# Two small SBUF regions of an mLSTM layer kernel moved to other byte addresses

## The chip, the cores and the metric

The kernel runs on one core of a Trainium2 chip. The metric is the device time of one execution in microseconds, lower being better. All data are float32; the large matmuls read their operands as fp32r, each value split into a high part and a low remainder, and three matmuls (high by low, high by high, low by high) stand for one product.

## The reference

One decoder layer of width 1024 over 2048 positions, cut to what is computed:

```python
u = rmsnorm(x, mix_norm_g)
q, k, v, o_pre, if_pre = split(u @ w_in)             # 1024 -> 512, 512, 1024, 1024, 16
h = mlstm(q, k, v, gates(if_pre))                    # 8 heads, matrix memory, chunk by chunk, with a stabiliser
y = (_rms(h) * norm_g * sigmoid(o_pre)) @ w_out
h = x + y
u = rmsnorm(h, ffn_norm_g)
out = h + (silu(u @ w_gate) * (u @ w_up)) @ w_down   # 1024 -> 2816 -> 1024
```

## The kernel before, in words

The sequence is worked in two halves of 1024 positions. Each half has four stages, one behind the other:

1. Projection. The normalised rows are turned and kept as `u_hi` and `u_lo`. The weight columns come in 12 groups; each group is seven products of a Strassen scheme (units), of 4 x 3 matmuls of 128x128 stationary weights by 512 moving columns. The weights of a unit stand in one of six slots, `pring`: ScalarE casts the high part from `raw` (L841), VectorE subtracts for the low part (L1280), TensorE multiplies (L1920, L1922, L1924). The gates' input is one more product, with the stationary `if_w` (L1938, 40 + 40 matmuls).
2. Chunks. Eight chunks of 128 positions go through the mLSTM recurrence in small matmuls (L2004 to L2105), and through the output projection with the stationary `hg_hi`, `hg_lo` and the moving `wo` (L1833 to L1835).
3. Feed. Gate and up projection, 11 groups of 14 units each, with the seven slots of `ring` as stationary operand and `u_hi`, `u_lo` or `t_op` as moving operand (L2179, L2181, L2182). Unit q uses slot q modulo 7. Slots are filled from `raw_f` (ScalarE L1107, VectorE L1671).
4. Drain. Down projection, 77 units of 12 matmuls (L2227, L2229, L2231). The stationary operand of unit e is slot e modulo 3, filled from `g_in` (ScalarE L1149, VectorE L1744), the moving one is slot 3 + e modulo 3, filled from the down weights (L1750).

Every tile has an address written out by hand. `region` hands out stretches of each partition in order, rounded up to 32 bytes, and tiles are placed at offsets in them:

```python
base = -(-nc.sbuf_base // 32) * 32
pring_at = [r_a + 12 * KB, r_q + 8 * KB, r_b + 8 * KB, r_q, r_q + 4 * KB, r_q + 12 * KB]
ring_at = [r_b + 8 * KB, r_b + 12 * KB, r_a + 12 * KB, r_q, r_q + 4 * KB, r_q + 8 * KB, r_q + 12 * KB]
t23_op = place("t23_op", r_c, [P, 2, 2, 4, NB], F32R)
```

The regions `r_u` (64 KB), `r_v` (33024 bytes) and `r_q` (33280 bytes) stand ahead of `r_a` (16 KB), `r_b` (16 KB) and `r_c` (32800 bytes), and behind these the small tiles (`state`, `ident`, `pick`, `mask` and others). `base` is 16512, which is 128 above a multiple of 256. All six regions start at 128 above a multiple of 256. Counted from `r_u` in units of 1024 bytes, `r_v` has the remainder 0, `r_q` 256, and `r_a`, `r_b` and `r_c` 768.

In `r_a` lie: the input rows `x_in` 1 to 3, `pring` slot 0, `negm`, `wint`, `cols`, `vtc`, `gain2`, `xn2`, `ring` slot 2 and three of the `kept` tiles. In `r_b`: `raw` 0, `pring` slot 2, `if_w`, `wo_raw`, half of `raw_f`, all of `g_in`, `ring` slots 0 and 1. The moving operands `u_hi` and `u_lo` lie in `r_u`, `t_op` in `r_c` and `r_v`.

Of the kernel before, what the change touches and what calls it, by code (L numbers as in the profile page):

```python
# [15 lines left out]
HEADS = 8  # L16
# [10 lines left out]
VW = DV + 1  # L27
# [94 lines left out]
def mlstm_layer(nc, x, mix_norm_g, ffn_norm_g, w_gate, w_up, w_down, w_in, b_if, norm_g, w_out, out):  # L122
# [8 lines left out]
    with ExitStack() as ctx:  # L131
# [6 lines left out]
        def region(nbytes):  # L138
            at = top[0]
            top[0] += -(-nbytes // 32) * 32  # L140
            return at
# [10 lines left out]
        KB = 1024  # L152
        r_u = region(64 * KB)
        r_v = region(TILES * HEADS * VW * 4)
        r_q = region(32 * KB + 512)
        r_a = region(16 * KB)
        r_b = region(16 * KB)
        r_c = region(28 * KB + HEADS * VW * 4)


        u_hi = place("u_hi", r_u, [P, TBS, KD, NB], F32R)
# [2111 lines left out]
```

## Time and profile before

| | before |
|---|---|
| median of 3 runs | 2180.55 us (2180.15 to 2181.9) |
| the profiled execution | 2179.42 us |
| its span, first to last instruction | 2177.8 us |
| TensorE busy | 2126.1 us, 98% |
| VectorE, ScalarE, GpSimd busy | 66%, 43%, 12% |
| mean granted TensorE clock | 0.994 |

The profiled execution is 1.6 us longer than its span (start and end outside the first and last instruction), and 1.1 us shorter than the median. The duration shown for a matmul contains its way through the pipeline; the pace of TensorE is to be read from the distances between starts.

### The profile page before, as it was taken

Reading aid. Unit: us, or ns where it says so; the run is one execution under the profiler, and the core shown is the slowest. Engines: PE = TensorE matmul, PEld = TensorE weight load, DVE = VectorE, ACT = ScalarE, POOL = GpSimd, SP = SyncE. Lnnn points to the kernel's source line nnn. Section 1 sums busy time; section 2 is a strip of 40 time slices with the busy share of each in tenths; the row PEclk is TensorE's granted clock in tenths of the full one; section 3 lists DMA queues with packets and bytes.
Section 4 is the critical chain, followed back from the end, with each engine's and each line's share of the span. In section 5 each row is a group of like instructions: output and inputs, shape, how many; then the busy total and the mean of one; then the engine's idle time right before and its main releaser. Section 6 shows DMA issues by size and latency. Waiting matters only on the chain.

```text
span 2177.8 us, 29479 instructions
## 1 busy us (share of the span) xinstructions
PE 2126.1 (98%) x10440; PEld 1766.0 (81%) x10440; DVE 1431.5 (66%) x2274; ACT 939.2 (43%) x1686; POOL 252.5 (12%) x357
## 2 busy tenths in 40 slices
PE   5999999999999999999999999899999999999999
PEld 4888878888888888788878888788888888888887
DVE  8775466686656565579687644767865756556764
ACT  4443664453333333345444346543533333333443
POOL 4111100020101010100122111001110101001000
PEclk8999999999999999999999999999999999999999
DMA  4333364213233324863524334532223332357443
GB/s 146 102 116 106 98 238 145 88 49 121 97 116 101 116 92 142 295 229 113 155 68 140 96 102 155 213 136 78 68 97 116 101 109 95 100 197 245 149 132 109
DMA packets 200289, 281.56 MB, mean 129 GB/s; under 512 B 12913, under 2 KB 131697, under 8 KB 200177
## 3 DMA queue, kind: packets, MB, share of 16 engines
q1 hardware_dynamic: 171696, 183.07, 26.6%
q0 software_dynamic: 28480, 97.02, 12.7%
q8 instruction: 68, 1.11, 0.2%
q14 instruction: 45, 0.36, 0.1%
HBM read 197.73 MB, written 82.31 MB: 129 GB/s over the span
## 4 chain that ended last, share of the span: by engine, by line
PE 89%; DVE 6%; ACT 2%; DMA 1%; issue 1%; SPq 0%; POOL 0%; DVEq 0%; POOLq 0%; ACTq 0%
PE ps L2179 13%; PE ps L2181 13%; PE ps L2182 13%; PE ps L1920 7%; PE ps L1924 7%; PE ps L1922 7%; PE ps L2227 6%; PE ps L2231 6%; PE ps L2229 6%; PE ps L1833 2%; PE ps L1835 2%; PE ps L1834 2%; PE ps L1840 1%; DMA g_in<-ops_hbm 1%; PE ps L2098 1%
## 5 line engine op out<-in xcount | busy, mean ns | idle before, releaser
L1671 DVE TENSOR_TENSOR ring<-raw_f,ring 128x512 fp32r<-128x512 f32 x308 | 211.4, 687 | 187.6 <-ACT ring L1107 186.5
L1107 ACT CAST ring<-raw_f 128x512 fp32r<-128x512 f32 x308 | 191.1, 622 | 208.0 <-PE ps L2182 194.0
L2179 PE MATMUL ps<-u_lo,ring 128*128 128x512 f32 x704 | 275.6, 391 | 2.2 <-DVE u_lo L1268 2.2
L2182 PE MATMUL ps<-u_hi,ring 128*128 128x512 f32 x704 | 274.1, 389 | 0.0
L2181 PE MATMUL ps<-u_hi,ring 128*128 128x512 f32 x704 | 273.9, 389 | 0.0
L2227 PE MATMUL ps<-ring,ring 128*128 128x512 f32 x616 | 240.9, 391 | 7.1 <-DVE ring L1750 7.1
L2229 PE MATMUL ps<-ring,ring 128*128 128x512 f32 x616 | 239.8, 389 | 0.0
L2231 PE MATMUL ps<-ring,ring 128*128 128x512 f32 x616 | 239.7, 389 | 0.0
L2179 PE MATMUL ps<-t_op,ring 128*128 128x512 f32 x528 | 205.9, 390 | 0.0
L2182 PE MATMUL ps<-t_op,ring 128*128 128x512 f32 x528 | 205.5, 389 | 0.0
L2181 PE MATMUL ps<-t_op,ring 128*128 128x512 f32 x528 | 205.4, 389 | 0.0
L1149 ACT CAST ring<-g_in 128x512 fp32r<-128x512 f32 x154 | 95.6, 621 | 223.3 <-PE ps L2231 210.4
L1744 DVE TENSOR_TENSOR ring<-g_in,ring 128x512 fp32r<-128x512 f32 x154 | 108.4, 704 | 110.5 <-ACT ring L1149 110.3
L772 POOL DMA_DIRECT2D ops_hbm<-kept x154 | 83.3, 541 | 761.3 <-DVE kept L1769 561.7
L1280 DVE TENSOR_TENSOR pring<-raw,pring 128x512 fp32r<-128x512 f32 x132 | 90.6, 690 | 110.0 <-ACT pring L841 109.2
L1764 DVE TENSOR_TENSOR kept<-ps,kept 128x512 f32<-128x512 f32 x132 | 90.9, 689 | 106.3 <-PE ps L2182 106.3
L2179 PEld LDWEIGHTS ps<-u_lo,ring 128*128 128x128 f32 x704 | 132.2, 188 | 29.6 <-DVE u_lo L1268 2.7
L2182 PEld LDWEIGHTS ps<-u_hi,ring 128*128 128x128 f32 x704 | 132.1, 188 | 27.6
L2181 PEld LDWEIGHTS ps<-u_hi,ring 128*128 128x128 f32 x704 | 132.2, 188 | 26.8
L1920 PE MATMUL ps<-u_lo,pring 128*128 128x512 f32 x384 | 151.1, 394 | 2.9 <-DVE u_lo L1268 2.8
L1924 PE MATMUL ps<-u_hi,pring 128*128 128x512 f32 x384 | 150.0, 391 | 0.0
L1922 PE MATMUL ps<-u_hi,pring 128*128 128x512 f32 x384 | 149.9, 390 | 0.0
(219 smaller groups left out, 4198.8 us busy)
## 6 DMA issues: line engine op xcount, KB each, us to landing
ops_hbm<-kept POOLq DMA_DIRECT2D x154, 256.0 KB, 2.4
g_in<-ops_hbm SPq DMA_DIRECT2D x154, 256.0 KB, 2.7
raw<-in_ml_w_in_dram SPq DMA_DIRECT2D x24, 1024.0 KB, 5.3
proj_hbm<-pkept POOLq DMA_DIRECT2D x96, 256.0 KB, 2.7
raw_f<-in_ffn_w_gate_dram SPq DMA_DIRECT2D x44, 512.0 KB, 4.7
raw_f<-in_ffn_w_up_dram SPq DMA_DIRECT2D x44, 512.0 KB, 4.5
b<-in_ffn_w_down_dram SPq DMA_DIRECT2D x88, 256.0 KB, 4.9
x_in<-in_x_dram SPq DMA_DIRECT2D x16, 512.0 KB, 6.1
```

The source lines that it names most:

```text
L1107: nc.scalar.copy(four(ring[slot][:, 0, :]), feed_source(q, s)).then_inc(w_hi_done, 1)
L1671: nc.vector.tensor_tensor(four(ring[slot][:, 1, :]), feed_source(q, s), four(ring[slot][:, 0, :].bitcast(F32)), ALU.subtract).then_inc(w_l ...
L1744: nc.vector.tensor_tensor(ring[e % 3][:, 1, :], g_in[e % 4][:, :], ring[e % 3][:, 0, :].bitcast(F32), ALU.subtract).then_inc(ea_lo_done, 1)
L1920: pe.matmul(banks(bank), w[:, 0, now], moved(kind, 1, k), start=(fresh and k == 0), stop=False, skip_group_check=True)
L1922: pe.matmul(banks(bank), w[:, 0, now], moved(kind, 0, k), start=False, stop=False, skip_group_check=True)
L1924: last = pe.matmul(banks(bank), w[:, 1, now], moved(kind, 0, k), start=False, stop=(k == 3), skip_group_check=True)
L2179: pe.matmul(banks(bank), wh, moved(kind, 1, k), start=(fresh and k == 0), stop=False, skip_group_check=True)
L2181: pe.matmul(banks(bank), wh, moved(kind, 0, k), start=False, stop=False, skip_group_check=True)
L2182: last = pe.matmul(banks(bank), wl, moved(kind, 0, k), start=False, stop=(k == 3), skip_group_check=True)
L2227: pe.matmul(banks(bank + j), a[:, 0, now], w[:, 1, :], start=(fresh and n == 0), stop=False, skip_group_check=True)
L2229: pe.matmul(banks(bank + j), a[:, 0, now], w[:, 0, :], start=False, stop=False, skip_group_check=True)
L2231: last = pe.matmul(banks(bank + j), a[:, 1, now], w[:, 0, :], start=False, stop=(n == GROUPS - 1), skip_group_check=True)
```

## The change

The starts of three regions are moved up by some bytes. Nothing else is changed: the same instructions, tiles, semaphores and orders.

```diff
-        r_a = region(16 * KB)
-        r_b = region(16 * KB)
-        r_c = region(28 * KB + HEADS * VW * 4)
+        r_a = region(192 + 16 * KB) + 192
+        r_b = region(96 + 16 * KB) + 96
+        r_c = region(224 + 28 * KB + HEADS * VW * 4) + 224
```

The paddings add up: `r_a` moves by 192 bytes, `r_b` by 192 + 96 = 288, `r_c` and every small tile behind it by 288 + 224 = 512. Counted modulo 256, `r_a` has moved by 192, `r_b` by 32, and everything else by nothing. With the regions move `ring` slots 0 and 1 (by 288), `ring` slot 2 (by 192), `pring` slot 2 and `if_w` (by 288) and `pring` slot 0 (by 192).

## Rows read from the trace of the kernel before

**Rows 1.** The page: its span, and part 1, busy time.

```profile
span 2177.8 us, 29479 instructions
...
PE 2126.1 (98%) x10440; PEld 1766.0 (81%) x10440; DVE 1431.5 (66%) x2274; ACT 939.2 (43%) x1686; POOL 252.5 (12%) x357
```

**Rows 2.** The page, part 4: the chain that ended last, by engine.

```profile
PE 89%; DVE 6%; ACT 2%; DMA 1%; issue 1%; SPq 0%; POOL 0%; DVEq 0%; POOLq 0%; ACTq 0%
```

**Rows 3.** Windows in feed and drain: us; busy and (instructions) by engine, clock, DMA.

```profile
500.00:600.00 100.00, 100.00 (x443) 82.81 (x442) 65.83 (x102) 36.75 (x63) 11.35 (x21) 1.00 0.29 96
...
1800.00:1900.00 100.00, 100.00 (x443) 82.81 (x442) 65.50 (x101) 36.37 (x62) 10.82 (x20) 1.00 0.29 94
1000.00:1080.00 80.00, 80.00 (x353) 65.74 (x352) 61.96 (x98) 39.57 (x76) 6.94 (x8) 1.00 0.49 147
2000.00:2100.00 100.00, 100.00 (x442) 82.78 (x442) 77.33 (x120) 42.26 (x74) 1.45 (x2) 1.00 0.44 137
```

**Rows 4.** Groups of TensorE instructions by line and form.

```profile
L2179 PE MATMUL ps<-u_lo,ring 128*128 128x512 f32 x704 | 275.6, 391 | 2.2 <-DVE u_lo L1268 2.2
...
L2227 PE MATMUL ps<-ring,ring 128*128 128x512 f32 x616 | 240.9, 391 | 7.1 <-DVE ring L1750 7.1
...
L2179 PE MATMUL ps<-t_op,ring 128*128 128x512 f32 x528 | 205.9, 390 | 0.0
...
L1920 PE MATMUL ps<-u_lo,pring 128*128 128x512 f32 x384 | 151.1, 394 | 2.9 <-DVE u_lo L1268 2.8
...
L1920 PE MATMUL ps<-t_op,pring 128*128 128x512 f32 x288 | 113.6, 394 | 5.4 <-DVE t_op L1268 5.3
...
L1833 PE MATMUL ps<-wo,hg_hi 128*128 128x512 f32 x256 | 103.6, 405 | 1.8 <-DVE wo L1488 1.8
...
L1938 PE MATMUL ps<-u_lo,if_w 128*128 128x512 f32 x40 | 16.0, 399 | 1.1 <-DVE u_lo L1268 1.1
```

**Rows 5.** Timeline of TensorE in the feed: start, duration, instruction.

```profile
599.61 0.39 PE L2179 MATMUL ps<-t_op,ring 128*128 128x512 f32 x1
...
600.97 0.39 PE L2179 MATMUL ps<-u_lo,ring 128*128 128x512 f32 x1
...
606.41 0.39 PE L2179 MATMUL ps<-t_op,ring 128*128 128x512 f32 x1
...
609.81 0.39 PE L2179 MATMUL ps<-t_op,ring 128*128 128x512 f32 x1
```

**Rows 6.** Timeline of TensorE in the drain.

```profile
999.73 0.39 PE L2229 MATMUL ps<-ring,ring 128*128 128x512 f32 x1
...
1009.92 0.39 PE L2229 MATMUL ps<-ring,ring 128*128 128x512 f32 x1
```

**Rows 7.** The tile ring: its weight loads, min/median/max ns.

```profile
L2179 PEld LDWEIGHTS ps<-u_lo,ring x704: 186/188/190, 461.3 to 1957.6; 128*128 128x128 f32 x176
...
L2227 PEld LDWEIGHTS ps<-ring,ring x616: 186/188/190, 889.1 to 2173.5; 128*128 128x128 f32 x154
```

**Rows 8.** Timeline of TensorE, small matmuls of two chunks.

```profile
344.55 2.05 PE L2098 MATMUL ps<-v,dmat 128*128 128x129 f32 x16
...
358.96 1.04 PE L2105 MATMUL ps<-ident,hrow 128*128 128x128 f32 x8
```

**Rows 9.** Line L1560 of VectorE, min/median/max ns.

```profile
L1560 DVE SCALAR_TENSOR_TENSOR state<-state,dec,ps x64: 339/344/352, 294.1 to 1503.1; 128x129 f32<-128x129 f32 x64
```

**Rows 10.** Who TensorE waited for, longest first.

```profile
PE ps L1840 <- DVE x_in L1244: 13.7, 4, 9.1
PE ps L2105 <- DVE hrow L1599: 8.6, 2, 4.3
PE ps L2227 <- DVE ring L1750: 7.1, 6, 2.4
```

**Rows 11.** The loads of g_in, L605: who waited, and us to landing.

```profile
  ACT ring L1149: 12.9, 2
...
DMA to landing us min/median/max: 2.4/2.7/14.6
```

**Rows 12.** The chain in a chunk stage, 285 to 440 us, by line.

```profile
by line: PE ps L1833 13.2%; PE ps L1835 13.0%; PE ps L1834 12.9%; PE ps L2098 7.7%; PE ps L2080 4.6%; PE ps L2105 4.4%; PE ps L2094 4.3%; PE ps L2016 3.5%; DVE wo L1488 3.1%; issue 2.5%; PE ps L2039 2.3%; PE ps L2004 2.1%; PE ps L2026 1.9%;
```

## The prediction

> **What bounds the kernel now.** I read the page first. TensorE is busy for 2126.1 us of a span of 2177.8 us [rows 1], and the chain that ended last is TensorE for 89% of the span, VectorE for 6%, ScalarE for 2% and DMA for 1% [rows 2]. So what counts first is the pace of TensorE, and only then what it waits for. The windows say the same by stage: in the feed and in the drain TensorE is busy without a gap, at a granted clock of 1.00 (2.4 GHz), with 442 or 443 instructions in 100 us [rows 3].
>
> The groups by line give the number of large matmuls. Each product is three lines with equal counts, of which I show one: feed 3 x (704 + 528) = 3696, drain 3 x 616 = 1848, projection 3 x (384 + 288) = 2016, output projection 3 x 256 = 768, and the gates 40 + 40 = 80 [rows 4]. That is 8408. Their pace comes from starts in the timeline: 45 distances in 599.61 to 609.81 us are 10.20 us, 226.7 ns each [rows 5]; 45 distances in the drain are 10.19 us, 226.4 ns [rows 6]. So 8408 x 0.2267 = 1906 us, 88% of the span, go at one pace. At 2.4 GHz it is 544 cycles for 512 columns. If a column takes a cycle (an estimate; no row shows less), 32 cycles, 13.3 ns, are left over in each matmul, and these are what an address could change on TensorE.
>
> **The change part by part.** No instruction, semaphore, order or byte count is changed, so there is nothing to add or take away by counting. What can change is the duration of an access whose address has another remainder. Every region began at the same remainder modulo 256. Now `r_a` is 192 off and `r_b` 32 off (and, `base` being a multiple of 64, starts no longer at a multiple of 64). I go through who touches them.
>
> *TensorE, stationary operand.* Moved are 6 of the 14 units of a feed group (slots 0, 1, 2, twice), 3696 x 6/14 = 1584 matmuls; all 1848 of the drain; 2 of 6 slots in the projection, 672; and the 80 of the gates: 4184 in all. In `r_b` are 1056 of the feed, 1248 of the drain (slots 0 and 1 in 52 of 77 units, 24 each), 336 and 80, together 2720. Of the moving operands of 512 columns none is moved modulo 256.
>
> What does the trace say of relative position? Only differences that are multiples of 256 occur among the large matmuls, but they differ among themselves. Modulo 512, `u_hi` and `u_lo` are 256 away from every `ring` slot, and `t23_op` (a part of `t_op`) is 0 away. The feed passes from `t_op` to `u_lo` and back: 6 distances on `t_op` take 1.36 us, the 24 that follow 5.44 us, the 15 after these 3.40 us, each 226.7 ns [rows 5]. The drain, whose two operands are 512 apart modulo 1024, has the same pace within 0.3 ns [rows 6]. A window of 100 us runs through all seven slots five times and has the same pace as one in the drain to 0.5% [rows 3]. The weight loads last 186 to 190 ns in all 704 and all 616 instances, whatever else ran [rows 7]. That is 38 ns less than the pace of 226.7 ns, so a load could grow by a fifth and still end under the matmul before it. A constant remainder of 32 cycles over all these pairs looks like a fixed price of a change of weights rather than like a collision that depends on low address bits. I cost this part at nothing.
>
> Both bounds of it: on the gain side all 13.3 ns on all 4184, that is 55.8 us. On the loss side the nearest row is one with starts off the usual grid, L2098, whose moving slices of 129 columns begin 516 bytes apart: 16 of them take 2.05 us, less the last one's 0.28 us is 1.77 us over 15 distances, 118 ns; the eight transposes of 128 columns with aligned operands take 1.04 - 0.27 = 0.77 us over 7, 110 ns [rows 8]. 8 ns more (one column and a change of pass are in it too) on the 2720 in `r_b` would be 21.8 us. Between nothing and these ends I take nothing, since the rows of the same form lie there.
>
> The row gives 226.7 ns from start to start. The Trainium skill, "TensorE: Matmul & The Clock Gate", section "Back-to-back issue gap", gives for an isolated matmul N/2.4 + 2.5 ns, 215.8 ns for 512 columns. The trace doesn't agree; were the 10.9 ns between them a collision that the shift ends, the sum would be 4184 x 10.9 ns = 45.6 us less, an estimate from that page. By the rows it is nothing.
>
> *VectorE and ScalarE.* They fill the moved slots and read `raw_f` 0, `g_in`, `raw` 0, `wo_raw`. VectorE is busy for 66% of a feed window and 77% of a drain window, ScalarE for about 37% and 42% [rows 3]; TensorE covers them, with slots filled ahead. Cover is gone only where a fill is waited for. TensorE's longest waits are 13.7 us for `x_in`, 8.6 us for `hrow` and 7.1 us for `ring` L1750 [rows 10]; of these `x_in` 1 to 3 and the `g_in` and slots behind the third are moved. In the chunk stage `wo` (reads `wo_raw`) is 3.1% of a chain of 155 us, 4.8 us, twice 9.6 us [rows 12]. What a start off the grid costs VectorE: the four slices of `state` are 516 bytes apart, and all 64 instances take 339 to 352 ns, 3.8% between the extremes [rows 9]. So 13.7 + 7.1 + 9.6 = 30.4 us x 3.8% = 1.2 us either way is the bound; I take 0.
>
> *DMA.* Loads of `g_in` land in 2.7 us at the median, 14.6 us at most (behind the down weights, at the start of a drain); ScalarE waits 12.9 us for them in two places [rows 11], of which TensorE feels a part of its 7.1 us. If a load to `r_b` were 5% slower, 0.05 x 14.6 = 0.7 us in each half, 1.5 us in all; I take 0.
>
> The trace doesn't split landing times by address. The Trainium skill, "DMA: Bandwidth & Descriptors", section "How a descriptor splits into AXI transactions", says that a descriptor not starting at a multiple of 256 bytes fetches from the boundary below it, in beats of 32 bytes. A row of 2048 bytes would take 68 beats before, 69 in `r_b` and 66 in `r_a`: an estimate of 0.2 us on the 14.6 us. Neither rule nor row makes more of it than noise.
>
> The sum: 2179.4 us of the profiled execution + 0 = 2179.4 us; with the 1.1 us by which the median lies above it, 2180.5 us.
>
> **The rivals.**
> 1. *The stationary reads collided with the moving ones and no longer do (faster).* For it: the 32 cycles left over, in a kernel whose operands all had one remainder modulo 256. Against it: the same pace at every multiple of 256 that occurs. Full price 55.8 us, 2124.7 us; a third of it, the likelier size as the collision would have to be partial, 18.6 us, 2161.9 us. It decides from 1.1 ns per matmul on. The weight loads might show it too.
> 2. *A start in `r_b` that is no multiple of 64 makes a weight load disturb the matmul beside it (slower).* For it: no weight load off that grid occurs before, so no row excludes it. Against it: the moving and VectorE rows at 516-byte steps. 8 ns x 2720 = 21.8 us, 2202.3 us; it decides from 1.6 ns per matmul on.
> 3. *Equal remainders were what kept the streams apart, and the shift makes them collide (slower).* Up to another 32 cycles on 4184, 2236 us. Nothing in the profile speaks for it but that other remainders are untried.
> 4. *The moved fills and landings make the waits longer (slower).* 1.2 + 1.5 = 2.7 us, 2183.2 us, which is still no measurable change; it would need 1.6 times its bound.
>
> **How the numbers follow.** A measurement of this kernel tells some 0.2%, 4.4 us, from no change. Forecast, no effect: 0.60 (rival 4 within it, 0.03 of it). Rival 1: 0.22. Rival 2: 0.13. Rival 3: 0.05. Faster 0.22, same 0.60, slower 0.18. The time is 2180.5 us; by itself the forecast's range is 2178 to 2183. For 8 in 10 I add the smaller half of rival 1 (down to 2158, 0.11) and the smaller part of rival 2 (up to 2192, 0.10), which makes 0.81.
>
> **What would show it.** In the changed kernel 45 distances in feed and drain should again be 10.2 us, and 100 us hold 442 or 443 instructions. Weight loads should stay at 188 ns. A distance other than 226.7 ns in the units of slots 0 to 2, with the old one in slots 3 to 6, would prove rival 1, 2 or 3; a drain that changed by more per matmul than the feed would too, since every unit of it is touched. Longer `L1107`, `L1671`, `L1149` or `L1744`, or longer landings of `g_in`, would be rival 4. I am wrong if low address bits matter at all to the pair of reads in TensorE: no row of this kernel tests that.

## The result, and the profile after

The changed kernel takes 2200.44 us (median of 3 runs, 2197.83 to 2202.06) against 2180.55 us: 0.88% slower, ratio 1.0088 (95% interval 1.0065 to 1.0111). The profiled execution takes 2202.06 us; its span is 2200.3 us, 22.5 us more than before. The forecast was 2180.5 us with a range up to 2192 us; the time lies above both.

The page after, its span and busy times, and of part 4 the line by engine:

```profile
span 2200.3 us, 29479 instructions
...
PE 2148.9 (98%) x10440; PEld 1768.0 (80%) x10440; DVE 1432.7 (65%) x2274; ACT 939.4 (43%) x1686; POOL 252.4 (11%) x357
...
PE 89%; DVE 6%; ACT 2%; DMA 2%; issue 1%; SPq 0%; POOL 0%; DVEq 0%; ACTq 0%; POOLq 0%
```

Beside [rows 1, 2]: the same 10440 matmuls keep TensorE busy for 22.8 us more, which is as much as the span has grown (22.5 us). VectorE has 1.2 us more, ScalarE 0.2 us, GpSimd nothing. The windows of the kernel after, with the columns of [rows 3]:

```profile
500.00:600.00 100.00, 100.00 (x438) 81.89 (x437) 65.61 (x101) 36.50 (x64) 10.81 (x20) 1.00 0.30 98
1000.00:1080.00 80.00, 80.00 (x346) 64.71 (x345) 63.81 (x103) 41.88 (x82) 5.47 (x6) 1.00 0.46 138
```

TensorE is again busy without a gap, at the same granted clock of 1.00, yet the feed window holds 438 matmuls where there were 443, and the drain window 346 where there were 353. So the matmuls themselves come at a slower pace: 1.1% in this feed window, 2.0% in this drain window. The groups by form show it weakly, since a duration contains the pipeline: after,

```profile
L2179 PE MATMUL ps<-u_lo,ring 128*128 128x512 f32 x704 | 277.6, 394 | 2.2 <-DVE u_lo L1268 2.2
L2227 PE MATMUL ps<-ring,ring 128*128 128x512 f32 x616 | 243.6, 395 | 7.7 <-DVE ring L1750 7.6
L2179 PE MATMUL ps<-t_op,ring 128*128 128x512 f32 x528 | 206.6, 391 | 0.0
...
L1833 PE MATMUL ps<-wo,hg_hi 128*128 128x512 f32 x256 | 103.5, 404 | 1.7 <-DVE wo L1488 1.7
```

means of 394, 395 and 391 ns where [rows 4] have 391, 391 and 390; L1833, whose operands did not change their remainders, stays (404 against 405). Sharper are the starts of units. In the feed after, the first matmul of the units of slots 0, 1, 2, 3, 4 and 5 of one group (timeline of TensorE), and in the drain of four units in a row, on slots 0, 1, 2 and 0:

```profile
627.00 0.39 PE L2179 MATMUL ps<-u_lo,ring 128*128 128x512 f32 x1
...
629.79 0.40 PE L2179 MATMUL ps<-u_lo,ring 128*128 128x512 f32 x1
...
632.59 0.40 PE L2179 MATMUL ps<-u_lo,ring 128*128 128x512 f32 x1
...
635.35 0.40 PE L2179 MATMUL ps<-u_lo,ring 128*128 128x512 f32 x1
...
638.09 0.39 PE L2179 MATMUL ps<-t_op,ring 128*128 128x512 f32 x1
...
640.81 0.39 PE L2179 MATMUL ps<-t_op,ring 128*128 128x512 f32 x1
...
981.64 0.40 PE L2227 MATMUL ps<-ring,ring 128*128 128x512 f32 x1
...
984.44 0.40 PE L2227 MATMUL ps<-ring,ring 128*128 128x512 f32 x1
...
987.24 0.39 PE L2227 MATMUL ps<-ring,ring 128*128 128x512 f32 x1
...
989.99 0.39 PE L2227 MATMUL ps<-ring,ring 128*128 128x512 f32 x1
```

Twelve matmuls take 2.72 us in slot 4, as everywhere before (12 x 226.7 ns), but 2.79 and 2.80 us in slots 0 and 1 (moved with `r_b`), 2.76 us in slot 2 (moved with `r_a`), and 2.74 us in slot 3, which did not move but follows slot 2. In the drain it is 2.80, 2.80 and 2.75 us. Over all units of the trace, the mean distance from start to start in ns, worked out from the starts in the two traces (distances over 300 ns left out):

```
              feed, slot 0    1      2      3      4      5      6     drain, slot 0  1      2      gates
before           226.8  226.8  226.8  226.8  226.8  226.7  226.8        226.8  227.0  226.8  227.5
after            232.8  233.4  229.6  228.5  226.8  226.7  227.5        233.0  233.2  229.9  233.1
```

The sum of these: feed (12.0 + 13.2 + 5.6 + 3.4 + 1.4 ns for the two units of each slot) x 12 x 22 groups = 9.4 us; drain 6.2 x 1248 + 3.1 x 600 = 9.6 us; projection 3.2 us in the same way; gates 0.4 us; 22.6 us in all, against 22.5 us of span. For this pair of executions nothing is left for anything else. The medians lie only 19.9 us apart, since the profiled execution before was 1.1 us below its median and the one after 1.6 us above; so a few us elsewhere, either way, are not excluded by this sum (e10 below does that). The other views agree. Weight loads after, then TensorE's waits, then landing times of `g_in`:

```profile
L2179 PEld LDWEIGHTS ps<-u_lo,ring x704: 186/188/190, 464.0 to 1973.3; 128*128 128x128 f32 x176
L2227 PEld LDWEIGHTS ps<-ring,ring x616: 186/188/192, 896.4 to 2196.0; 128*128 128x128 f32 x154
```

```profile
PE ps L1840 <- DVE x_in L1244: 13.6, 4, 9.3
PE ps L2105 <- DVE hrow L1599: 8.6, 2, 4.3
PE ps L2227 <- DVE ring L1750: 7.6, 5, 2.6
```

```profile
DMA to landing us min/median/max: 2.4/2.7/13.7
```

The loads' durations [rows 7] and the landing at its least and median [rows 11] are as they were, the three waits [rows 10] to 0.5 us; the longest landing is 0.9 us shorter. A weight load is not longer on record; what is stretched is the distance between matmuls.

### The profile page after: what moved, and what is told of

Its sections match the earlier page's. It is cut to its first block, busy times and chain, and to the rows that moved or that the text cites. A ratio compares the mean times of both kernels' runs of the same rounds, so it can differ in the third digit from the quotient of the medians.

```text
span 2200.3 us, 29479 instructions
## 1 busy us (share of the span) xinstructions
PE 2148.9 (98%) x10440; PEld 1768.0 (80%) x10440; DVE 1432.7 (65%) x2274; ACT 939.4 (43%) x1686; POOL 252.4 (11%) x357
## 4 chain that ended last, share of the span: by engine, by line
PE 89%; DVE 6%; ACT 2%; DMA 2%; issue 1%; SPq 0%; POOL 0%; DVEq 0%; ACTq 0%; POOLq 0%
PE ps L2182 13%; PE ps L2179 13%; PE ps L2181 13%; PE ps L1920 7%; PE ps L1922 7%; PE ps L1924 7%; PE ps L2227 6%; PE ps L2231 6%; PE ps L2229 6%; PE ps L1833 2%; PE ps L1835 2%; PE ps L1834 2%; PE ps L1840 1%; DMA g_in<-ops_hbm 1%; PE ps L2098 1%
## 5 line engine op out<-in xcount | busy, mean ns | idle before, releaser
L1671 DVE TENSOR_TENSOR ring<-raw_f,ring 128x512 fp32r<-128x512 f32 x308 | 211.5, 688 | 192.6 <-ACT ring L1107 192.3
L1107 ACT CAST ring<-raw_f 128x512 fp32r<-128x512 f32 x308 | 190.9, 622 | 213.1 <-PE ps L2182 205.1
L2227 PE MATMUL ps<-ring,ring 128*128 128x512 f32 x616 | 243.6, 395 | 7.7 <-DVE ring L1750 7.6
L2231 PE MATMUL ps<-ring,ring 128*128 128x512 f32 x616 | 243.0, 395 | 0.0
L2229 PE MATMUL ps<-ring,ring 128*128 128x512 f32 x616 | 243.0, 394 | 0.0
L1149 ACT CAST ring<-g_in 128x512 fp32r<-128x512 f32 x154 | 95.5, 620 | 232.5 <-PE ps L2231 218.2
L1744 DVE TENSOR_TENSOR ring<-g_in,ring 128x512 fp32r<-128x512 f32 x154 | 108.5, 705 | 119.3 <-ACT ring L1149 119.0
```

The source lines that it names most:

```text
L1107: nc.scalar.copy(four(ring[slot][:, 0, :]), feed_source(q, s)).then_inc(w_hi_done, 1)
L1671: nc.vector.tensor_tensor(four(ring[slot][:, 1, :]), feed_source(q, s), four(ring[slot][:, 0, :].bitcast(F32)), ALU.subtract).then_inc(w_l ...
L1744: nc.vector.tensor_tensor(ring[e % 3][:, 1, :], g_in[e % 4][:, :], ring[e % 3][:, 0, :].bitcast(F32), ALU.subtract).then_inc(ea_lo_done, 1)
L2227: pe.matmul(banks(bank + j), a[:, 0, now], w[:, 1, :], start=(fresh and n == 0), stop=False, skip_group_check=True)
L2229: pe.matmul(banks(bank + j), a[:, 0, now], w[:, 0, :], start=False, stop=False, skip_group_check=True)
L2231: last = pe.matmul(banks(bank + j), a[:, 1, now], w[:, 0, :], start=False, stop=(n == GROUPS - 1), skip_group_check=True)
```

## The experiments

Theory A: what counts is where the stationary operand of a large matmul lies. In form A1 it is its place relative to the moving operand, modulo some power of two; in form A2 the start of the operand itself, against a grid. Theory B: the fills and transfers into the moved regions are slower. Each ratio is to the kernel before, timed on the same chip, and the microseconds behind a ratio are worked out from it (the medians alone give 41 us for e4 and within 1 us of the figure given for the others). Diffs are against the kernel before; `...` stands for lines left out. Paces of slots are means over the distances between starts in the trace, as above.

**e1_rb32**: only `r_b` is moved modulo 256.

```diff
-        r_b = region(16 * KB)
-        r_c = region(28 * KB + HEADS * VW * 4)
+        r_b = region(32 + 16 * KB) + 32
+        r_c = region(224 + 28 * KB + HEADS * VW * 4) + 224
```

> Only r_b is moved by 32 bytes modulo 256 (the small tiles behind it by 256). Theory A, the address of the stationary operand sets TensorE's pace: the units of ring slots 0 and 1 go at 233 ns per matmul as in the changed kernel, slot 2 and all others at 226.7 ns; in all 528 x 12.8 ns in the feed, 1248 x 6.3 ns in the drain, 336 x 6.5 ns in the projection and 0.5 us for the gates, 17.3 us above the kernel before (ratio 1.008). Theory B, fills and transfers into the region are slower and TensorE waits: the pace stays 226.7 ns and the waits grow.

Measured: 2197.5 us, ratio 1.0071 (1.0055 to 1.0088), 15.5 us where 17.3 were expected. Feed slots 0 and 1 at 232.8 and 233.4 ns, slots 2 to 5 at 226.6 to 227.2 ns, drain slots 0 and 1 at 232.8 and 233.4 ns. The last distance in a unit of slot 6, the one ahead of the first matmul of slot 0, is 235 ns (226.7 ns before). The timeline shows what runs in it: the last matmul of slot 6 on `t_op`, the load of the first weights of slot 0, then their matmul.

```profile
625.46 0.40 PE L2182 MATMUL ps<-t_op,ring 128*128 128x512 f32 x1
625.47 0.19 PEld L2179 LDWEIGHTS ps<-u_lo,ring 128*128 128x128 f32 x1
625.70 0.39 PE L2179 MATMUL ps<-u_lo,ring 128*128 128x512 f32 x1
```

So the cost begins one matmul early, at the time when the first moved weights are loaded beside an unmoved matmul. The stationary operands in `r_b` alone (two `ring` slots, one `pring` slot and `if_w`) make most of the loss.

**e2_ra192**: only `r_a` is moved modulo 256.

```diff
-        r_a = region(16 * KB)
-        r_b = region(16 * KB)
+        r_a = region(192 + 16 * KB) + 192
+        r_b = region(64 + 16 * KB) + 64
```

> Only r_a is moved by 192 bytes modulo 256 (r_b and the small tiles by 256). Theory A: ring slot 2 goes at about 229.5 ns and the first matmuls of slot 3 too, pring slot 0 likewise; 2.4 us in the feed, 1.6 us in the drain, 0.9 us in the projection, 4.9 us above the kernel before (ratio 1.002). A variant of A in which only starts off a multiple of 64 cost: no change at all, ratio 1.000, since 192 is a multiple of 64.

Measured: 2183.58 us, ratio 1.0012 (1.0002 to 1.0021), 2.6 us. Slot 2 goes at 229.0 ns, its distances run 229, 232, 226 in turn; all others, slot 3 too, at 226.7 to 227. So a start that is moved by a multiple of 64 costs as well, if less, and the grid of 64 of the second rival is not the explanation. The two together (18.1 us) agree with the change (19 us by its ratio) within the intervals; slot 3, slow in the changed kernel (228.5 ns) and in neither of these two, would make 0.9 us of the difference.

**e3_all32**: everything is moved by 32 bytes.

```diff
-        base = -(-nc.sbuf_base // 32) * 32
+        base = -(-nc.sbuf_base // 32) * 32 + 32
```

> All regions and tiles together are moved by 32 bytes, so that no operand's position relative to another changes, but every start is off a multiple of 64. Theory A1, the position of the stationary operand relative to the moving one counts: pace 226.7 ns everywhere, ratio 1.000. Theory A2, the start of the stationary operand itself counts: all 8408 large matmuls pay the 6.3 ns seen in the slots of r_b, 53 us more, ratio 1.024 or above if the moving operand pays as well.

Measured: 2181.65 us, ratio 1.0006 (0.9997 to 1.0016), and the windows in feed and drain, first of the kernel before, then of this one:

```profile
560.00:660.00 100.00, 100.00 (x443) 82.81 (x442) 60.63 (x93) 37.32 (x64) 9.42 (x18) 1.00 0.33 105
960.00:1060.00 100.00, 100.00 (x441) 82.27 (x441) 83.91 (x136) 52.87 (x102) 5.48 (x6) 1.00 0.56 180
...
560.00:660.00 100.00, 100.00 (x443) 82.84 (x442) 60.39 (x93) 37.34 (x64) 9.11 (x17) 1.00 0.33 105
960.00:1060.00 100.00, 100.00 (x441) 82.30 (x440) 83.89 (x136) 52.87 (x102) 5.46 (x6) 1.00 0.56 182
```

Every operand stands 32 bytes off and nothing is slower. A2 falls; A1 stands.

**e4_scan**: one kernel with a different shift for each slot (`pring` and `if_w` likewise; the tiles behind them in `r_q` are moved by 256).

```diff
-        ring_at = [r_b + 8 * KB, r_b + 12 * KB, r_a + 12 * KB, r_q, r_q + 4 * KB, r_q + 8 * KB, r_q + 12 * KB]
+        ring_at = [r_b + 8 * KB + 64, r_b + 12 * KB + 128, r_a + 12 * KB + 96, r_q + 32, r_q + 4 * KB + 160,
+                   r_q + 8 * KB + 192, r_q + 12 * KB + 224]
...
```

> Each ring slot has its own shift modulo 256 while the moving operands of the feed stay: slot 0 64, slot 1 128, slot 2 96, slot 3 32, slot 4 160, slot 5 192, slot 6 224 bytes. The pace of each slot in the feed is read from the trace. Theory A1 with a period of 64 bytes: slots 0, 1 and 5 at 226.7 ns, slots 2, 3, 4 and 6 at 233 ns; since 192 cost 2.7 ns in the changed kernel the period should be longer, and then the slots take several paces, slot 5 about 229.5 ns and slot 3 about 233 ns. If any slot is faster than 226.7 ns, there is a version that beats the kernel before. The time is expected 30 to 60 us above before.

Measured: 2222.25 us, ratio 1.020 (1.018 to 1.022), 44 us.

```profile
560.00:660.00 100.00, 100.00 (x432) 80.70 (x431) 55.81 (x86) 36.44 (x63) 8.14 (x15) 1.00 0.32 103
960.00:1060.00 100.00, 100.00 (x430) 80.44 (x429) 82.50 (x136) 50.41 (x96) 1.47 (x2) 1.00 0.55 175
```

Every slot is slow, those at 64, 128 and 192 bytes too, so a period of 64 bytes falls. The next kernel adds finer steps, and its table has the paces of both.

**e6_fine**: the slots are views that begin some elements into their tile.

```diff
-        ring_at = [r_b + 8 * KB, r_b + 12 * KB, r_a + 12 * KB, r_q, r_q + 4 * KB, r_q + 8 * KB, r_q + 12 * KB]
-        ring = [place(f"ring{i}", at, [P, 2, NB], F32R) for i, at in enumerate(ring_at)]
+        ring_at = [r_b + 8 * KB + 224, r_b + 12 * KB + 224, r_a + 12 * KB, r_q, r_q + 4 * KB,
+                   r_q + 8 * KB, r_q + 12 * KB]
+        ring_off = (4, 7, 3, 1, 2, 4, 6)
+        ring = [place(f"ring{i}", at, [P, 2 * NB + 8], F32R)[:, o:o + 2 * NB].rearrange("p (a n) -> p a n", a=2)
+                for i, (at, o) in enumerate(zip(ring_at, ring_off))]
...
```

> Steps finer than 32 bytes: ring slot 0 is 240 bytes off modulo 256, slot 1 252, slot 2 12, slot 3 4, slot 4 8, slot 5 16, slot 6 24 (pring likewise). If what counts are pieces of 32 bytes, slots 2 to 6 stay at 226.7 ns and slots 0 and 1 go at 233 ns like 224. If any difference from 0 counts, all are slower, up to 233 ns. If a slot is faster than 226.7 ns, some of the 32 cycles above 512 are a collision that the kernel before still has; I expect none. Between 6 and 45 us more.

Measured: 2213.13 us, ratio 1.0147 (1.0129 to 1.0165), 32 us. The pace of the feed by the place of the stationary operand relative to the moving one, from the starts in both traces (fifth to eleventh distance of a unit, so that the neighbour slots weigh little), with 0 from the kernel before:

```
bytes modulo 256   0     4     8     12    16    24    32    64    96    128   160   192   224   240   252
ns per matmul    226.7 232.3 230.5 233.2 233.3 230.1 232.7 233.6 234.2 232.3 233.8 229.0 233.1 228.3 233.3
```

Zero is the only place without a cost. There is no order in the rest that I can name: 4 bytes cost 5.6 ns, 192 bytes cost 2.3 ns. None is faster than 226.7 ns. So the reading in pieces of 32 bytes falls, and the other, that any difference costs, stands. The figures are good to about 1 ns: 32 bytes reads 232.7 here and 233.3 in e8.

The drains of these two kernels have pairs in which both operands are moved. In e4 their differences are 32, 224 and 160 bytes, and the same seven distances read 233.1, 233.2 and 234.4 ns, as in the feed. In e6 they are 236 (stationary at 240, moving at 4), 244 (252 and 8) and 252 (12 and 16), and read 236.6, 231.1 and 230.3 ns, where 252 in the feed reads 233.3. So at steps of 32 bytes the difference gives the cost to about 1 ns, but at finer steps it does not give it alone; no run moves the moving operand by less than 32 bytes while the stationary one stays.

**e5_ru32**: the moving operand is moved instead.

```diff
-        r_u = region(64 * KB)
-        r_v = region(TILES * HEADS * VW * 4)
+        r_u = region(32 + 64 * KB) + 32
+        r_v = region(224 + TILES * HEADS * VW * 4) + 224
```

> Only r_u, in which the moving operands u_hi, u_lo and wo lie, is moved by 32 bytes modulo 256; no stationary operand and no ring slot is. Theory A1, the position of the stationary relative to the moving operand counts (here -32, that is 224, for which the scan showed 233 ns): the units on u_hi and u_lo go at about 233 ns in all seven slots, those on t_op and the whole drain at 226.7 ns, the output projection slower too; 4112 matmuls x 6.4 ns = 26 us more, ratio 1.012. Rival: only the place of the stationary operand counts: ratio 1.000.

Measured: 2208.95 us, ratio 1.0128 (1.011 to 1.0147), 28 us. Windows in feed and drain:

```profile
560.00:660.00 100.00, 100.00 (x434) 81.18 (x433) 55.62 (x85) 36.63 (x63) 8.12 (x15) 1.00 0.32 103
960.00:1060.00 100.00, 100.00 (x442) 82.58 (x441) 84.44 (x138) 50.58 (x97) 1.47 (x2) 1.00 0.56 182
```

The feed has 434 instead of 443, the drain is untouched. By unit: 233.3 to 233.6 ns in each of the eight of a group on `u_lo` and `u_hi`, whichever slot; of the six on `t_op`, 226.7 to 226.8 in those that follow another on `t_op`, 229.7 in those that come right behind a unit on `u_lo`. The output projection, on `wo`, goes from 228.4 to 233.1 ns. No slot was moved, and the slots are slow. The last distance of a unit on `t_op`, the one ahead of the first matmul on `u_lo`, is 226.7 ns: in it the next weights are loaded beside a moving operand that stands at the same remainder as they do.

**e7_pad256**: shifts of 256, 512 and 768 bytes.

```diff
-        r_a = region(16 * KB)
-        r_b = region(16 * KB)
-        r_c = region(28 * KB + HEADS * VW * 4)
+        r_a = region(256 + 16 * KB) + 256
+        r_b = region(256 + 16 * KB) + 256
+        r_c = region(256 + 28 * KB + HEADS * VW * 4) + 256
```

> r_a is moved by 256, r_b by 512, r_c by 768 bytes: other addresses and other places modulo 512 and 1024, but all operands have equal remainders modulo 256. Theory A1 with a period of 256: pace 226.7 ns everywhere, ratio 1.000. With a longer period (512 or 1024): the feed and the drain slower, by up to 6.5 ns on 4184 matmuls, 27 us.

Measured: 2180.5 us, ratio 1.0000 (0.9990 to 1.0010); all slots of feed and drain at 226.6 to 227.1 ns. Moves by whole multiples of 256 bytes cost nothing.

**e8_slots32**: all slots are moved by 32 bytes.

```diff
+        ring_at = [r_b + 8 * KB + 32, r_b + 12 * KB + 32, r_a + 12 * KB + 32, r_q + 32, r_q + 4 * KB + 32,
+                   r_q + 8 * KB + 32, r_q + 12 * KB + 32]
...
```

> All seven ring slots, all pring slots, if_w and one of the three hg tiles are moved by 32 bytes modulo 256, the moving operands in r_u, r_v and r_c are not. In the drain both operands are ring slots, so their relative position stays. Theory A1: feed and projection at 233 ns in every slot, the drain back at 226.7 ns, although its stationary operands stand exactly where the changed kernel has two of them; (3696 + 2016 + 80 + 288) x 6.3 ns = 38 us more, ratio 1.0176. Rival, the stationary start itself counts: the drain at 233 ns too, 50 us, ratio 1.023.

Measured: 2216.94 us, ratio 1.0164 (1.0146 to 1.0182), 36 us. Windows in feed and drain:

```profile
560.00:660.00 100.00, 100.00 (x431) 80.49 (x430) 55.56 (x86) 36.01 (x62) 8.14 (x15) 1.00 0.33 104
960.00:1060.00 100.00, 100.00 (x442) 82.56 (x441) 83.64 (x138) 51.22 (x98) 1.47 (x2) 1.00 0.56 179
```

431 in the feed, 442 in the drain. The stationary operands of the drain stand where the change put two of them, but their moving partners now stand there too, and the pace is 226.9 ns.

**e10_slots_back**: the changed kernel with the stationary operands put back and everything else in `r_a` and `r_b` left shifted.

```diff
-        r_a = region(16 * KB)
-        r_b = region(16 * KB)
+        r_a = region(192 + 16 * KB + 64) + 192
+        r_b = region(32 + 16 * KB + 224) + 32
-        ring_at = [r_b + 8 * KB, r_b + 12 * KB, r_a + 12 * KB, r_q,
+        ring_at = [r_b + 8 * KB + 224, r_b + 12 * KB + 224, r_a + 12 * KB + 64, r_q,
...
```

> The changed kernel, but with ring slots 0 to 2, pring slots 0 and 2 and if_w (with t4, which shares its place) put back to the remainder of the moving operands; raw, raw_f, g_in, wo_raw, x_in, xn2, negm, wint, cols, vtc and the kept tiles stay shifted by 32 or 192 bytes modulo 256. Theory A1, only the pair of the large matmuls' operands counts: 226.7 ns everywhere, ratio to the kernel before 1.000 (within 0.2%). Rival, the fills, transfers or small matmuls in the shifted regions hold a part of the loss: the sum of e1 and e2 (18.1 us) against the slots' 22 us leaves them at most a few us, ratio up to 1.002.

Measured: 2180.86 us, ratio 0.9995 (0.9986 to 1.0004). Windows in feed and drain:

```profile
560.00:660.00 100.00, 100.00 (x443) 82.86 (x442) 60.42 (x93) 36.83 (x64) 8.66 (x16) 1.00 0.33 105
960.00:1060.00 100.00, 100.00 (x441) 82.30 (x441) 84.11 (x136) 52.16 (x101) 5.47 (x6) 1.00 0.56 184
```

The counts are those of the kernel before. Fills, transfers and small matmuls with shifted operands cost at most 0.04% (0.9 us) by the upper end of the interval. B falls.

**e9_small_even**: the kernel before with the small tiles at the common remainder.

```diff
-        r_c = region(28 * KB + HEADS * VW * 4)
+        r_c = region(28 * KB + HEADS * VW * 4 + 224)
...
         state = small("state", [P, 4, VW])
+        region(224)
         colt = small("colt", [P, TILES, 72])
```

> The kernel before with state, colt, ident, ident_b, pick, mask and not_first moved so that they begin at the remainder of all regions too (before: 160 for state, 192 for the others, against 128). If the pair rule holds for the small matmuls of 128 columns, transposes (ident against x_in, hrow, vtc) and L2004, L2026 get cheaper; their pace of 109 ns is likely set by something else, since 192 against 128 costs nothing visible there. Expected between 0 and 3 us less, ratio 0.999 to 1.000; a gain of over 4 us would make it a version better than both.

Measured: 2179.92 us, ratio 0.9995 (0.9986 to 1.0004). No gain beyond the noise. The transposes L1840 and L2105, with `ident` 64 bytes off their other operand before and 0 here, have a median distance of 109 ns in both traces: they don't pay for this difference. Nothing in these experiments points to a version that beats the kernel before.

## Why the prediction was wrong

*What bounds the kernel* was right: the pace of TensorE in 8408 matmuls of 512 columns decides, and it did.

*TensorE, stationary operand* is the step that failed: "I cost this part at nothing", because the pace was the same for all pairs that the kernel has. All of these pairs lie a multiple of 256 bytes apart, as I had noted, and e7 shows that such pairs are alike. They were samples of one case, not of many; the argument from them to other differences had nothing under it, as the prediction's own last sentence says ("no row of this kernel tests that"). The runs put 19.9 us in its place by the medians, 22.6 us by the trace: 5.6 to 6.6 ns on each of 2720 matmuls at 32 bytes (16.8 us), 2.3 to 3.1 ns on 1464 at 192 bytes (4.1 us), and 1.7 us on unmoved units next to these. The count of 4184 affected matmuls was right, and e5 and e8 show that it was right to ask whether a moving operand moves too. The drain changed by more per matmul than the feed (5.2 against 2.5 ns), which the prediction had named as a sign of a real effect in TensorE; its slots 3 and 6 did not keep the old pace as it said, since each stands next to a moved one.

The 32 cycles in excess of 512 were read as a fixed price of a change of weights. In fifteen places tried none had less, so nothing contradicts that, and nothing shows it either. But it said nothing about what could come on top: 5.6 to 7.5 ns, 13 to 18 cycles at 2.4 GHz, at ten of the fourteen differences of the table, and 1.6 to 3.8 ns at the other four.

*Rival 2* had nearly the size (21.8 us against 20 measured), by luck: it wanted a start off a multiple of 64 to cost by itself, which e3 excludes, and had 8 ns from rows of matmuls of another form. *Rival 3*, equal remainders keep the two streams apart, is the one that e3, e5 and e8 bear out; I gave it 0.05 and its full price, 32 more cycles, where the runs show 13 to 16 at 32 bytes and 5 to 7 at 192. *Rival 1* is excluded at every place tried: no mean pace went below 226.7 ns. *Rival 4* is excluded by e10, and the fills' medians are the same before and after (L1107 622 ns, L1671 686 ns, L1149 621 ns, L1744 692 ns). The sentence that the weight loads could grow by a fifth unseen was beside the point: the loads stayed at 188 ns on record and the matmuls were stretched.

*VectorE and ScalarE*, *DMA*: nothing, as said. L1560 after takes 340 to 351 ns, as in [rows 9], and in e10 the fills with shifted operands cost nothing. By the Trainium skill, "DMA: Bandwidth & Descriptors", section "How a descriptor splits into AXI transactions", 0.2 us were at stake, the prediction's estimate. That is too little for these runs to see, and the section speaks of what is fetched, whereas the moved end of these loads is the one written. The 10.9 ns between the 215.8 ns of the Trainium skill, "TensorE: Matmul & The Clock Gate", section "Back-to-back issue gap", and the row were no collision to be won back at any shift tried.

What stays open: which part of the chip the two reads share. That the read of the next matmul's weights and the moving read of the present one disturb each other is argued, not shown. For it speak the ends of the moved units: in e1 the cost begins in the distance in which the first moved weights are loaded (235 ns), and in e5 there is none yet in the last distance before the moving operand changes (226.7 ns). Against a simple form of it speak the distances that stay long behind a moved unit, and the drain of e6, where the difference alone does not give the cost. No run took the loads away from beside the matmuls. Open is also why the distances in the traces add up to somewhat more than the times differ in the other slow kernels: 18.4 us against 15.5 in e1, 46.5 against 44 in e4, 37.3 against 32 in e6, 38.5 against 36 in e8. Executions of one kernel differ by 2 to 8 us, and each trace is one execution.

## What to carry to other kernels

Where TensorE streams large fp32r matmuls back to back, place the stationary and the moving operands of the matmuls that follow each other at the same remainder modulo 256 bytes, and keep every padding and tile size in between a multiple of 256: a region that grows by 32 bytes in front of a weight buffer can cost 3% of the pace of each matmul that uses it. Padding by 256, 512 and 768 bytes cost no time (e7). No run here shows the rule for other types or for weights kept over several matmuls. When a trace shows one pace for all pairs of operands, first ask what these pairs have in common before taking it as proof that their places don't matter. Such a loss shows in no wait and no load; it shows in the distance between starts, and in how many matmuls fit in 100 us.

## What was not expected of the hardware

At a granted clock of 1.00, fp32r matmuls of 128x128 by 512 columns, each with its own weights, start 226.7 ns apart when both operands have equal remainders modulo 256 bytes, and 228.3 to 234.2 ns apart at each of fourteen other differences in the feed, down to 4 bytes (up to 236.6 ns in the drain of e6); moving both operands together by 32 bytes changes nothing (ratio 1.0006), nor do 256, 512 or 768 bytes (1.0000). The slow pace is not even: at 32 bytes distances of 235 and 231.6 ns alternate, at 192 bytes 229, 232 and 226 follow each other, and after a move back to an equal remainder the first few distances are still uneven (in e5 the first of such a unit is 241 ns, the second 224, and from the eighth on they are 226.7). The rule did not show in the transposes of 128 columns, 109 ns apart whether their operands' remainders are equal or 64 bytes apart (e9).
